# Gate and up products of 18 of 22 FFN tiles as seven block products, with two of the four weight sums made by GpSimd

## What is computed

```
def swiglu(h, w_gate, w_up, w_down):
    return (jax.nn.silu(h @ w_gate) * (h @ w_up)) @ w_down

for l in range(DEPTH):                      # DEPTH = 2
    x = x + 0.5 * swiglu(rms_norm(x, ffn1_norm[l]), ffn1_w_gate[l], ...)
    ...
    x = x + 0.5 * swiglu(rms_norm(x, ffn2_norm[l]), ffn2_w_gate[l], ...)
    x = rms_norm(x, final_norm[l])
```

## Time and profile before

| | |
|---|---|
| median of 3 runs | 2427.04 us |
| lowest and highest | 2423.78, 2427.71 us |
| span of the profiled execution | 2422.0 us |
| TensorE busy | 2388.1 us, 99% |
| VectorE busy | 1268.0 us, 52% |
| ScalarE busy | 923.1 us, 38% |
| GpSimd busy | 28.5 us, 1% |
| granted TensorE clock, mean | 0.999 |

### The profile page before, as it was taken

The page is one execution under the profiler, slowest core; times in us unless marked ns, Lnnn a source line. Parts: engine busy times, 40 slices in busy tenths (PEclk is TensorE's granted clock), DMA queues, the critical chain, the costliest instruction groups (busy, mean ns, idle before and its releaser), DMA issues.

```text
span 2422.0 us, 35922 instructions
## 1 busy us (share of the span) xinstructions
PE 2388.1 (99%) x14420; PEld 1921.9 (79%) x14420; DVE 1268.0 (52%) x2017; ACT 923.1 (38%) x1425; POOL 28.5 (1%) x28
## 2 busy tenths in 40 slices
PE   8999999999999999999999999999999999999998
PEld 6888888856788888888888888667888888779687
DVE  5434454568664344574344445686543446583564
ACT  4222233477432222332122245774322224452623
POOL 2000000000000000020000000000000000000000
PEclk9999999999999999999999999999999999999999
DMA  7233333200233333343333332002333333322001
GB/s 229 81 99 106 88 94 98 81 1 19 70 87 93 98 102 86 106 122 93 100 102 84 106 98 64 19 2 72 102 87 95 104 88 118 96 87 70 2 4 70
DMA packets 322769, 201.43 MB, mean 83 GB/s; under 512 B 9888, under 2 KB 313984, under 8 KB 322272
## 3 DMA queue, kind: packets, MB, share of 16 engines
q1 hardware_dynamic: 322112, 195.68, 27.9%
q0 software_dynamic: 544, 4.18, 0.5%
HBM read 197.74 MB, written 2.10 MB: 83 GB/s over the span
## 4 chain that ended last, share of the span: by engine, by line
PE 93%; DVE 3%; ACT 2%; DVEq 1%; issue 0%; DMA 0%; ACTq 0%; SPq 0%
PE bank L906 74%; PE bank L1095 4%; PE bank L1126 2%; PE bank L1078 2%; PE bank L1139 2%; PE bank L1186 2%; PE bank L1431 1%; PE bank L1041 1%; PE bank L1053 0%; DVE top L2573 0%; DVE bank L2579 0%; DVEq L2558 0%; DVEq L2595 0%; PE bank L1051 0%; DVE spare_hi L2564 0%
## 5 line engine op out<-in xcount | busy, mean ns | idle before, releaser
L906 PE MATMUL bank<-h_hi,w_hi 128*128 128x512 f32 x1568 | 612.4, 391 | 0.3 <-DVE w_lo L2761 0.2
L906 PE MATMUL bank<-h_hi,w_lo 128*128 128x512 f32 x1568 | 610.1, 389 | 0.0
L906 PE MATMUL bank<-h_lo,w_hi 128*128 128x512 f32 x1568 | 610.1, 389 | 0.0
L2178 DVE TENSOR_TENSOR w_lo<-raw,w_hi 128x2048 fp32r<-128x2048 f32 (+2 forms) x197 | 407.5, 2069 | 163.4 <-ACT w_hi L1618 161.3
L1618 ACT CAST w_hi<-raw 128x2048 fp32r<-128x2048 f32 (+2 forms) x198 | 340.6, 1720 | 386.6 <-PE bank L906 344.9
L906 PEld LDWEIGHTS bank<-h_hi,w_hi 128*128 128x128 f32 x1568 | 294.3, 188 | 66.8 <-issue 5.0
L906 PEld LDWEIGHTS bank<-h_hi,w_lo 128*128 128x128 f32 x1568 | 294.3, 188 | 61.3
L906 PEld LDWEIGHTS bank<-h_lo,w_hi 128*128 128x128 f32 x1568 | 294.3, 188 | 60.7 <-issue 0.2
L1659 ACT ACTIVATE probs<-probs 128x512 f32<-128x512 f32 x88 | 55.6, 632 | 686.7 <-DVE probs L2271 686.7
L906 PE MATMUL bank<-hid_hi,w_hi 128*128 128x512 f32 x704 | 273.9, 389 | 0.0
L906 PE MATMUL bank<-hid_lo,w_hi 128*128 128x512 f32 x704 | 273.9, 389 | 0.0
(11 more groups left out here) (436 smaller groups left out, 2642.7 us busy)
## 6 DMA issues: line engine op xcount, KB each, us to landing
raw<-in_ffn_w_up SPq DMA_DIRECT2D x88, 512.0 KB, 5.2
raw<-in_ffn_w_gate SPq DMA_DIRECT2D x87, 512.0 KB, 4.0
raw<-in_w_in SPq DMA_DIRECT2D x60, 512.0 KB, 4.5
raw<-in_ffn_w_down SPq DMA_DIRECT2D x64, 384.0 KB, 4.0
raw<-in_ffn_w_down SPq DMA_DIRECT2D x64, 320.0 KB, 3.4
raw<-in_w_out SPq DMA_DIRECT2D x24, 512.0 KB, 4.5
na_bias<-in_na_rel POOLq DMA_DIRECT2D x2, 1792.0 KB, 9.6
raw<-in_w_in SPq DMA_DIRECT2D x8, 416.0 KB, 3.7
```

Of the source, the lines that this page charges most:

```text
L906: last = pe.matmul(to, left[a](k), right[b](k), start=(begin and k == 0 and a + b == 0), stop=(end and k == n - 1 and a == 1))
L2178: dve.tensor_tensor(w_lo[:, at, 0:n], raw[:, at, 0:n], w_hi[:, at, 0:n].bitcast(F32), ALU.subtract)\
```

## The change

An FFN's tiles are now in four chunks of 4, 6, 6 and 6, each followed by its down products. The 4 tiles of the first chunk are made as before. The 18 others are made by Winograd's form of Strassen's algorithm: the weights of a tile are seen as a 2 x 2 matrix of blocks (gate and up by lower and upper half of k; `A11`, `A12`, `A21`, `A22`, 512 elements per partition each), the operand as 2 x 2 blocks (half of k by half of the tokens), and instead of eight block products there are seven, each of 4 k and 256 tokens: 12 matmuls of 256 columns. For this four sums of weight blocks are needed in each tile (`S1` to `S4`), and four sums of operand blocks (`N1`, `N2`, `T3`, `T4`) in each FFN.

- *GpSimd* (`block_sums_of`): A11 + A21 into `sums`, and A21 + A22 over A21 in `raw`. It waits for the panel to land and, since `sums` exists once, for VectorE's part 1 of the tile before.
- *VectorE*: two more sums, then the splits in four parts (`block_second`: 1024, 1024, 1024, 512 elements), the up sum (`seven_up`), the hidden tile in one instruction (`seven_hid`), `hid_lo`. A tile's own splits are done while TensorE works on the tile before. Since the operand sums need the norm's root, `normed_rows` and `mix_operands` are done during the plain tiles.
- *ScalarE*: the casts in four parts (`block_first`), and four copies of 256 columns out of PSUM (`first_copy_of`, `second_copy_of`, `third_copy_of`): partial sums that enter two results are copied to a second place and added to by the next product there.
- *TensorE* (`seven_tiles`): for each tile `first`, then `up` and `last` of the tile before, `second`, `seventh`, `gate`, `third`. `first` of a chunk's first tile stands before down d=7 of the chunk before, and three k of down d=0 before `up` and `last` of a chunk's last tile.
- *Down products* (`down_all`): over 4 or 6 hidden tiles, so 12 or 18 matmuls for each d; four panels of two d each (two panels of four d after the first chunk); banks 5 to 7 in turn. d = 0 and 1 are interleaved: both up to the last k, then the last k of each.
- *Memory*: `more_lo`, `sums` and the operand blocks lie over `na_bias` and `t5_bias`. So GpSimd loads both in every layer, after the last tile of FFN 1, and adds the mask then.
- The loops over tiles are written out.

The core of the diff:

```diff
+PLAIN = 4
+CHUNKS = (PLAIN, 6, 6, 6)
+DOWN_W = [4 * P, 2 * P, 2 * P, 2 * P]
...
+            def block_sums_of(l, f):
+                for j in range(PLAIN, KF):
+                    i = ffn_first(f) + tile_panel(j)
+                    at = slot(l, i)
+                    pool.wait_ge(raw_loaded[at], (used(l, i) + 1) * 32)
+                    pool.wait_ge(part_split, split_at(l, f, T4) if j == PLAIN else split_at(l, f, j=j - 1, part=1))
+                    a11, _, a21, a22 = (raw[:, at, b * BLOCK:(b + 1) * BLOCK] for b in range(4))
+                    pool.tensor_tensor(sums[:, 1, :], a11, a21, ALU.add)
+                    pool.drain()
+                    pool.tensor_tensor(a21, a21, a22, ALU.add).then_inc(pool_summed, 1)
...
+                block_sums_of(l, 1)
+                pool.wait_ge(gate_up_done, hid_at(l, 1, KF))
                 pool.dma_start(na_bias[:, :, :], A["na_rel"][l]).then_inc(layer_loaded, 16)
+                pool.dma_start(t5_bias[:, :, :], A["t5_rel"]).then_inc(layer_loaded, 16)
...
+            def seven(l, f, j, to, a, b, begin=False):
+                at = slot(l, ffn_first(f) + tile_panel(j))
+                w_hi_, w_lo_, x_hi, x_lo = weights(j, at, a), weights(j, at, a, True), operand_part(b), operand_part(b, True)
+                for k in range(HALF_K):
+                    pe.matmul(columns_at(to), w_hi_[:, k, :], x_hi[:, k, :], start=(begin and k == 0), stop=False, skip_group_check=True)
+                    pe.matmul(columns_at(to), w_hi_[:, k, :], x_lo[:, k, :], start=False, stop=False, skip_group_check=True)
+                    last = pe.matmul(columns_at(to), w_lo_[:, k, :], x_hi[:, k, :], start=False, stop=(k == HALF_K - 1),
+                                     skip_group_check=True)
+                return last
...
+            def tile_second(l, f, j):
+                pe.wait_ge(part_split, split_at(l, f, j=j, part=1))
+                pe.wait_ge(sums_copied, copied_at(l, f, "first", j))
+                seven(l, f, j, gate_later(j), S2, N2).then_inc(products_done, 1)
...
+            def down_all(l, f, c, begun=0):
+                n = CHUNKS[c]
+                down(l, f, c, 0, range(begun, n - 1))
+                down(l, f, c, 1, range(n - 1))
+                down(l, f, c, 0, [n - 1])
+                down(l, f, c, 1, [n - 1])
+                for d in range(2, KD):
+                    if d == KD - 1 and c < len(CHUNKS) - 1:
+                        tile_first(l, f, CHUNK_AT[c + 1])
+                    down(l, f, c, d, range(n))
...
+            def block_first(l, f, j, part):
+                i = ffn_first(f) + tile_panel(j)
+                at = slot(l, i)
+                if j == CHUNK_AT[chunk_of(j)] or j - 1 == CHUNK_AT[chunk_of(j)]:
+                    c = chunk_of(j) - 1
+                    d = (KD // DOWN_PANELS[c]) * (DOWN_PANELS[c] - 1 + j - CHUNK_AT[c + 1]) - 1
+                    act.wait_ge(down_done, down_at(l, f, c, d) + 1)
...
+            def block_sums_of(l, f, j):
+                i = ffn_first(f) + tile_panel(j)
+                at = slot(l, i)
+                dve.wait_ge(pool_summed, pool_at(l, f, j))
+                a12, a22 = (raw[:, at, b * BLOCK:(b + 1) * BLOCK] for b in (1, 3))
+                dve.drain()
+                dve.tensor_tensor(sums[:, 0, :], sums[:, 1, :], a22, ALU.add)
+                dve.drain()
+                dve.tensor_tensor(sums[:, 2, :], sums[:, 0, :], a12, ALU.add).then_inc(part_summed, 1)
```

More of the change, by code:

```diff
@@ L895, in spread_roots, with product @@
                 last.then_inc(spread_done, 1)
-            def product(to, left, right, n, ready=None, hid=None, begin=True, end=True):
+            def product(to, left, right, n, ready=None, begin=True, end=True):
                 for k in range(n):
@@ L902, in product @@
                         pe.wait_ge(h_ready, ready + k + 1)
-                    if hid is not None and k in (0, n - 1):
-                        pe.wait_ge(hid_ready, hid - 1 if k == 0 else hid)
                     for a, b in ((0, 0), (0, 1), (1, 0)):
@@ new lines, in tile_last, with seven_tiles @@
+            def tile_last(l, f, j):
+                split(l, ffn_first(f) + tile_panel(j))
+                seven(l, f, j, gate_later(j), S4, B22).then_inc(gate_up_done, 1)
+            def seven_tiles(l, f, c):
+                first, last = CHUNK_AT[c], CHUNK_AT[c] + CHUNKS[c] - 1
+                for j in range(first, last + 1):
+                    if j > first:
+                        tile_first(l, f, j)
+                        tile_up(l, f, j - 1)
+                        tile_last(l, f, j - 1)
+                    tile_second(l, f, j)
+                    tile_seventh(l, f, j)
+                    tile_gate(l, f, j)
+                    tile_third(l, f, j)
+                begun = 3
+                down(l, f, c, 0, range(begun))
+                tile_up(l, f, last)
+                tile_last(l, f, last)
+                down_all(l, f, c, begun)
@@ new lines, in ffn @@
+                n, q, next_ = ffn_norm(l, f)
+                if n == 0:
+                    first_gate_up()
+                else:
+                    gate_up(l, first, 0, hid_at(l, f, 0), ready=operand(l, c), between=lambda: sums_of_squares(n, next_))
+                spread_roots(q, next_ is not None)
+                for j in range(1, PLAIN):
+                    gate_up(l, first + tile_panel(j), j % 2, hid_at(l, f, j))
+                down_all(l, f, 0)
+                pe.wait_ge(down_added, down_at(l, f, 0, 4) + 1)
@@ L989, in project @@
+                for c in range(1, len(CHUNKS)):
+                    seven_tiles(l, f, c)
             def project(l):
@@ new lines, in ffn @@
+                late_second(l, f, B11)
+                late_second(l, f, T4)
+                for d in range(2):
+                    down_add(l, f, 0, d)
+                for j in range(2):
+                    ks = slice(HALF_K + 2 * j, HALF_K + 2 * j + 2)
+                    last = operand_second(l, f, B21 + j, h_lo[:, ks, :], late_rows[j][:, :, :], h_hi[:, ks, :])
+                last.then_inc(part_split, 1)
+                for d in (2, 3):
+                    down_add(l, f, 0, d)
+                block_sums_of(l, f, PLAIN)
```

613 lines of the change are left out of this document (434 added, 179 removed).

## The result

The changed kernel takes 2436.9 us (median; 2432.0 to 2448.0) against 2428.2 us for the kernel before in the same rounds: a ratio of 1.0039, 95% interval 1.0024 to 1.0054. The forecast was 2421, slightly faster. The profiled execution spans 2435.7 us, against 2422.0. Some executions of most of the kernels here, the one before too, are 10 to 17 us longer at a lower mean granted clock; "like for like" means the medians without them, here 2435.2 (12 of 20) against 2427.4 us (16 of 20).

A forecast was written before the change was run, and what follows sets the result against it. TensorE, busy 99% of the span, was taken as the bound. 58.3 us saved less new waits of 19.2, 11.6, 13.4 and 8.0 left 6.1 us faster: a span of about 2416, so 2421 us; range 2406 to 2450.

The forecast's parts named there:

- pace of 72 tiles: Block-product tiles of the four FFNs: 10.08 us of TensorE each against 10.89, 58.3 us saved.
- chunk heads, 12: TensorE's second product waits for ScalarE's copy, queued behind the next tile's part-0 cast: 1.6 us each, 19.2 us.
- end of the plain tiles, 4: TensorE's down products after the plain tiles wait for hid_lo of tile 3: 2.9 us each, 11.6 us.
- end of FFN 2, twice: VectorE falls behind the down products; TensorE waits 4.7 us for the next panel, 2.3 for h_lo: 13.4 us in all.
- end of FFN 1, twice: TensorE waits 0.5 us, plus 3.5 from mask adds beside VectorE's work: 4.0 per FFN, 8.0 us.
- The loop's cycle: Steady tiles: GpSimd and VectorE need 10.3 us against TensorE's 10.08; covered by 2.1 us a chunk, so costing nothing.
- The price of a third add: GpSimd making the first of its two adds twice in each tile: 38 to 55 us more, 2475 to 2492.
- the mask adds' share: End of FFN 1: eight GpSimd mask adds beside VectorE's work on k=3 to 6 add some 3.5 us.
- less time for which it newly waits: The prediction's sum: what counts is time TensorE no longer needs, less its new waits.
- the rivals: Besides the largest: waits are cheaper, 2414 (20%) or 2388 (5%); block products are no faster, 2479 (5%).
- GpSimd and VectorE as the bound: Six-tile chunks: the pair's cycle exceeds 10.7 us and TensorE waits; 2438 or 2454, slower; chance 28%.

The follow-up runs named there:

- five: `all_four` plus the second copy of a chunk's first tile made before ScalarE's part-2 cast; 2403.1 us, ratio 0.9885 to the kernel before.
- filled: Changed kernel with useless TensorE matmuls in its longest waits, at the ends of the FFNs and of the plain tiles; 2434.6 us.
- slow_before: Kernel before, without block products, with VectorE splitting the next stage's first panel three times over at each FFN's end; 2456.2 us, ratio 1.0098.
- mask_later: Changed kernel with GpSimd's eight mask adds waiting until VectorE is through with the end of FFN 1; 2426.0 us.
- tail_light: Changed kernel without VectorE's multiplication by the gain at FFN ends: ScalarE makes h_hi straight from xT, VectorE h_lo in one instruction; 2423.6 us.
- all_four: Changed kernel with first copy before the cast at chunk heads, later mask adds, no gain on VectorE at FFN ends, hid_lo before the down split; 2407.3 us.
- hid_before: Changed kernel with hid_hi and hid_lo of the last plain tile made before the down split of 2048 elements; 2423.9 us.

## Why the prediction was wrong

The direction was wrong; most terms were near, and one that matters was missing. By the starts in TensorE's timeline:

| term | forecast | measured |
|---|---|---|
| pace of 72 tiles | 58.3 saved | 57.2 |
| chunk heads, 12 | 19.2 | 19.9 |
| end of the plain tiles, 4 | 11.6 | 11.7 (2.6, 2.4, 4.4, 2.4) |
| plain tiles themselves | 0 | 2.9, in one FFN |
| end of FFN 2, twice | 13.4 | 8.9 |
| end of FFN 1, twice | 8.0 | 7.5 |
| half clock after waits | no term | 14 |
| start of the program | no term | 2.4 |

- **Pace.** Right: 10.08 us a tile, no wait inside the chunks. Between tiles and down products 0.09 us a chunk are lost.
- **The loop's cycle.** VectorE's was forecast at 10.3, and is 9.8. That it costs nothing was right. The price of a third add was forecast at 38 to 55 us and is 13 to 15, because the cycle began further below TensorE's.
- **Chunk heads, plain ends, FFN 1.** Right in place and size, the mask adds' share too: 3.5 us forecast, 4.2 found. The sum over the plain ends is luck: I took one price, 2.9, for all four, where three are 2.4 to 2.6 and one is 4.4. In the second layer's FFN 1 VectorE has the final norm's output to make in the same tiles:

```profile
1068.20 5.39 DVE L2554 SCALAR_TENSOR_TENSOR xT<-xT,cols,mixed 128x512 f32<-128x512 f32 x8
```

  Its eight instructions of 0.75 us were there before, and TensorE did not wait; now they stand ahead of the mixing, and TensorE waits 2.9 us for a split and 4.4 for hid_lo. `five` still waits there for 2.5 and 2.9.
- **End of FFN 2.** Forecast 4.7 and then 2.3; found 4.1 and then 0 and 0.65. With the first wait filled (`filled`) the second is 2.0, near the forecast: the slow TensorE had hidden it. The waits together, 50.9 us against 52.2, are nearer than they deserve: this term was 4.5 us too high, and 2.9 us in the plain tiles had none.
- **The failed step** is the sum itself: "less time for which it newly waits" took a wait at its own length and put the half clock behind it at nothing. It costs 14 us in the changed kernel's trace, more than the 6.1 us that the forecast had left, and `slow_before` shows 17.3 us of waits costing 27.3. The 52 us of waits that the prediction counted lie in pieces of 1.7 us at the chunk heads, behind which no stretch at half clock stands in any trace here, and in pieces of 2.4 to 4.4, nine in the changed kernel's trace, of which six have one. The profile of the kernel before could not show it, since its clock is 0.999, but it could have made me ask: its longest wait in the FFNs is 0.4 us. The page "TensorE: Matmul & The Clock Gate" of the Trainium skill (section "HAM oscillation — how this bites in real kernels") describes a kernel whose TensorE waits between bursts and then runs the next burst at the lower clock; the traces here agree (idle for 3.7 us, then 6.8 us at half clock, at 375 us), and the prediction should have weighed it as a rival.
- **Start.** The first product begins 2.4 us later (23.09 against 20.68 us). 2.1 us of it are the clock as well (the other 0.3 a later landing of the input): TensorE's first matmuls of 512 columns stand 0.43 us apart in the changed kernel's trace where they stand 0.23 apart in that of the kernel before, since full clock was granted at 16.1 us in the one and at 9.6 in the other:

```profile
12.14 0.63 PE L1100 MATMUL bank<-h_lo,w_hi 128*128 128x512 f32 x1
...
12.57 0.63 PE L1101 MATMUL bank<-h_hi,w_lo 128*128 128x512 f32 x1
```

  It is not the change: `slow_before`, with the start of the kernel before, has it too, and `mask_later`, with the start of the changed one, has not. It moves from one execution to another.

The balance: -57.2 + 50.9 + 14 + 2.4, less 0.8 us of waits that the kernel before had, is 9 us; the spans differ by 13.7. Some 4 us are not placed. They lie in no one stage: compared stage by stage, from first matmul to first matmul, none has more than 0.7 us of them. (One slip in the forecast's own sum: 7.0 less 0.4 is 6.6, not 6.7, at each FFN 2.)

None of the rivals came true. The largest, GpSimd and VectorE as the bound (28%), is refuted by the steady tiles.

## What to carry to other kernels

When a change to a kernel that keeps TensorE busy throughout brings waits of a few microseconds, price them above their length: first the time itself, then the matmuls that may follow at half clock (0.8 to 3.3 us a stretch here), unless another engine is behind there anyway. A wait can be cheap to remove when it is only an order: a copy behind a cast, adds of another engine that could run later. And a saving of 58 us was real here; it was lost at the seams, and five small repairs brought back 34 us.

## What the runs showed of the hardware

Whether the granted clock falls behind a wait is partly chance: behind the same waits of 2.4 to 2.6 us at the end of the plain tiles it fell in `mask_later` (at 67 and 723 us) and stayed up in the changed kernel (69 and 731 us). Two waits of 1.7 and 1.1 us some 6 us apart, at the end of FFN 2, were enough at one of the two FFN 2 in `tail_light` and `all_four`, and at both in `five`. Behind a single wait of 1.66 us it never fell, in 84 chunk heads of seven traces.

One stretch is of another kind: in the traces of `hid_before` and `five` the second block has 34.1 us at half clock. Both begin at the same place, 0.7 and 0.1 us behind the second of two waits of 0.6 us that stand 2.1 us apart; the ten other traces have these two waits and no such stretch, so what sets it off stays open. Within it TensorE is busy throughout, in `five`:

```profile
2314.90:2349.00 34.10, 34.10 (x302) 24.78 (x303) 11.70 (x33) 11.16 (x57) 0.00 (x0) 0.50 0.10 32
...
2350.00:2380.00 30.00, 30.00 (x138) 24.90 (x137) 16.61 (x22) 8.27 (x10) 0.00 (x0) 1.00 0.11 36
```
